# Four stationary columns for the conditioning products, all-ones input norm sums, filter operands padded to 128 rows

## What is computed

```python
def rms_norm(x, gain):
    xf = x.astype(jnp.float32)
    y = xf * lax.rsqrt(jnp.mean(xf * xf, axis=-1, keepdims=True) + NORM_EPS)
    return (y * gain.astype(jnp.float32)).astype(x.dtype)
...
def adaln(cond, ada_w, ada_b):
    m = jax.nn.silu(cond) @ ada_w + ada_b
    return jnp.split(m, 3, axis=-1)
...
    hid = jnp.sin(feats @ w1 + b1)
    hid = jnp.sin(hid @ w2 + b2)
    taps = (hid @ w3 + b3).reshape(L, 2, HY_ORDER, HY_WIDTH)
...
    yn = ((yf - mean) * lax.rsqrt(var + RWKV_GN_EPS)).reshape(y.shape[:2] + (BRANCH_W,))
    yn = (yn * gn_w + gn_b).astype(v.dtype)
```

## Time and profile before

| | |
|---|---|
| median of three runs | 3252.37 us (3250.11 to 3253.16) |
| the profiled execution | 3250.34 us, span 3248.5 us |
| PE busy | 2901.3 us, 89% |
| DVE busy | 1540.9 us, 47% |
| ACT busy | 1063.6 us, 33% |
| POOL busy | 62.1 us, 2% |
| moved by DMA | 243.24 MB, mean 75 GB/s |

### The profile page before, as it was taken

One profiled execution on the slowest core, in us unless ns is written; L12 is line 12 of the kernel. 1 busy time (PEld: TensorE's weight loads), 2 busy tenths in 40 slices (PEclk: granted clock), 3 DMA queues, 4 the chain that ended last, 5 costly groups with the idle time before them and its releaser, 6 DMA issues. The chain is left out here.

```text
span 3248.5 us, 53541 instructions
## 1 busy us (share of the span) xinstructions
PE 2901.3 (89%) x23122; PEld 2232.8 (69%) x23122; DVE 1540.9 (47%) x2528; ACT 1063.6 (33%) x1886; POOL 62.1 (2%) x69
## 2 busy tenths in 40 slices
PE   7899889989986888788999999799887988899997
PEld 3588656867855777346788777566656876788876
DVE  5623347353546555556555224454536435354522
ACT  6411357232242333212222222454324133322221
POOL 0000000000000122000000000000000000000000
PEclk9899999989976999698999999899988998899999
DMA  9411200124125111301232223222211112223321
GB/s 314 120 59 52 43 1 2 52 76 131 33 58 146 46 50 33 107 19 46 79 99 95 91 76 107 89 60 66 59 52 55 40 58 92 72 75 94 97 85 65
DMA packets 250172, 243.24 MB, mean 75 GB/s; under 512 B 28248, under 2 KB 218200, under 8 KB 249873
## 3 DMA queue, kind: packets, MB, share of 16 engines
q1 hardware_dynamic: 249634, 238.64, 23.7%
q10 hardware_dynamic: 304, 1.18, 0.1%
HBM read 217.03 MB, written 22.24 MB: 74 GB/s over the span
## 5 line engine op out<-in xcount | busy, mean ns | idle before, releaser
L212 DVE TENSOR_TENSOR second_w_low<-second_w_raw,second_w_high 128x1024 fp32r<-128x1024 f32 (+1 forms) x236 | 282.3, 1198 | 486.8 <-ACT second_w_high L208 486.0
L208 ACT CAST second_w_high<-second_w_raw 128x1024 fp32r<-128x1024 f32 (+1 forms) x236 | 241.6, 1025 | 681.0 <-PE ffn_in_acc L233 248.5
L231 PE MATMUL ffn_in_acc<-ffn_h_high,second_w_high 128*128 128x512 f32 x704 | 280.9, 399 | 7.7 <-DVE ffn_h_low L674 5.8
L233 PE MATMUL ffn_in_acc<-ffn_h_high,second_w_low 128*128 128x512 f32 x704 | 278.2, 395 | 0.0
L232 PE MATMUL ffn_in_acc<-ffn_h_low,second_w_high 128*128 128x512 f32 x704 | 278.2, 395 | 0.0
L212 DVE TENSOR_TENSOR first_w_low<-first_w_raw,first_w_high 128x1024 fp32r<-128x1024 f32 x91 | 110.7, 1223 | 248.2 <-ACT first_w_high L208 248.0
L208 ACT CAST first_w_high<-first_w_raw 128x1024 fp32r<-128x1024 f32 x91 | 94.7, 1047 | 208.5 <-PE attn_in_acc L233 80.7
L231 PEld LDWEIGHTS ffn_in_acc<-ffn_h_high,second_w_high 128*128 128x128 f32 x704 | 133.9, 190 | 39.6 <-issue 9.9
L231 PE MATMUL attn_in_acc<-attn_h_high,first_w_high 128*128 128x256 f32 (+1 forms) x416 | 144.3, 347 | 14.4 <-DVE attn_h_low L406 14.4
L232 PEld LDWEIGHTS ffn_in_acc<-ffn_h_low,second_w_high 128*128 128x128 f32 x704 | 134.0, 190 | 29.6 <-issue 0.7
L233 PEld LDWEIGHTS ffn_in_acc<-ffn_h_high,second_w_low 128*128 128x128 f32 x704 | 133.8, 190 | 29.7
(11 more groups left out here) (817 smaller groups left out, 6353.1 us busy)
## 6 DMA issues: line engine op xcount, KB each, us to landing
second_w_raw<-in_ffn_w_gate SPq DMA_DIRECT2D x44, 512.0 KB, 3.5
second_w_raw<-in_ffn_w_up SPq DMA_DIRECT2D x44, 512.0 KB, 3.6
second_w_raw<-in_ffn_w_down SPq DMA_DIRECT2D x40, 512.0 KB, 3.4
first_w_raw<-in_rec_w_in SPq DMA_DIRECT2D x33, 512.0 KB, 3.8
second_w_raw<-in_w_in SPq DMA_DIRECT2D x24, 512.0 KB, 3.8
second_w_raw<-in_w_branch_gate SPq DMA_DIRECT2D x24, 512.0 KB, 3.8
first_w_raw<-in_attn_w_in SPq DMA_DIRECT2D x22, 512.0 KB, 3.7
first_w_raw<-in_attn_ada_w SPq DMA_DIRECT2D x12, 512.0 KB, 8.4
```

What stands on the lines that cost most here:

```text
L208: act.copy(self.view(self.high[b % self.splits], b), self.view(self.raw[self.ring[b]], b)).then_inc(self.high_done, 1)
L212: dve.tensor_tensor(self.view(self.low[b % self.splits], b), self.view(self.raw[self.ring[b]], b), self.view(self.high[b % self.splits], b ...
L231: pe.matmul(out, sh, mh, start=(first and j == 0), stop=False)
L233: ins = pe.matmul(out, sl, mh, start=False, stop=(last and j == len(parts) - 1))
```

## The change

Three things change, and one moves with them.

The diff, cut to its core:

```diff
@@ class InputRoots
     def begin(self, st):
-        self.root = Root(self.nc, st, self.c, self.root_out, ring=4)
         self.squares = [st.sb(f"squares{i}", [P, TT]) for i in range(4)]
-        self.spread = st.ps("root_spread", [P, 2 * BANK])
+        self.sums = st.ps("root_sums", [P, 2 * BANK])
+        self.squared, self.summed, self.rooted = (st.sem("root_" + n) for n in ("squared", "summed", "rooted"))
...
-        if step == 16:
-            self.root.take(act)
-        if step == 22:
-            self.root.keep(act, self.spread[:, 0:TT])
...
+        if step == 17:
+            act.wait_ge(self.summed, KD)
+            act.activation(self.root_out, self.sums[:, 0:TT], ACT.Sqrt, bias=self.c["eps"]).then_inc(self.rooted, 1)
 
     def pe(self, pe, step):
-        if 8 <= step < 8 + KD:
-            self.root.add(pe, step - 8, self.squares[(step - 8) % 4])
-        if step == 19:
-            self.root.spread_over(pe, self.spread)
+        k = step - 8
+        if 0 <= k < KD:
+            pe.wait_ge(self.squared, k + 1)
+            for t0, tn in spans(TT, BANK):
+                ins = pe.matmul(self.sums[:, t0:t0 + tn], self.c["ones"], self.squares[k % 4][:, t0:t0 + tn],
+                                start=(k == 0), stop=(k == KD - 1))
+            ins.then_inc(self.summed, 1)
 
     def dve(self, dve, step):
-        if step == 18:
-            self.root.make_diag(dve)
+        if step in (18, 20, 22):
+            at = slice(128 * (step - 18), 128 * (step - 16))
+            dve.wait_ge(self.rooted, 1)
+            dve.reciprocal(self.root_out[:, at], self.root_out[:, at])
@@ def linear_tokens
+                    if stacked:
+                        half, out = slice(t0, t0 + rows // 2), ps[n % slots][:, 0:sum(widths)]
+                        for j, k in enumerate(ks):
+                            pe.matmul(out[0:rows], x(k)[:, at], high[:, j, :], start=(k == 0), stop=False, skip_group_check=True)
+                            ins = pe.matmul(out[0:rows // 2], x(k)[:, half], low[:, j, :], start=False, stop=(k == kc - 1),
+                                            skip_group_check=True)
+                        ins.then_inc(product_done, 1)
+                        continue
@@ def adaln
-        rows = keep.enter_context(nc.sbuf_tensor("adaln_rows", [2, len(layers) * 3 * D], F32))
-        high, low = (keep.enter_context(nc.sbuf_tensor("adaln_cond_" + n, [P, KD, 2], F32R)) for n in ("high", "low"))
+        rows = keep.enter_context(nc.sbuf_tensor("adaln_rows", [4, len(layers) * 3 * D], F32))
+        parts = keep.enter_context(nc.sbuf_tensor("adaln_cond_parts", [P, KD, 4], F32R))
+        high, low = parts[:, :, 0:2], parts[:, :, 2:4]
...
-                        ins = pe.transpose(ps[:, i, n, :], rows[:, at:at + P], ident[0:2, 0:2])
+                        ins = pe.transpose(ps[:, i, n, :], rows[:, at:at + P], ident[0:4, 0:4])
...
                         chain.link(dve.tensor_tensor(mod[:, :, j], ps[:, i, :, j], bias, ALU.add))
+                        chain.link(dve.tensor_tensor(mod[:, :, j], mod[:, :, j], ps[:, i, :, 2 + j], ALU.add))
@@ def hidden_loads (new), def filter_loads
+    tables = {"hidden": Ahead(nc, keep, "filt_hidden")}
+    for n, src, shape in (("w1", "hy_w1", [33, 64]), ("w2", "hy_w2", [64, 64]), ("feats", "c_feats", [33, S])):
+        tables[n] = keep.enter_context(nc.sbuf_tensor("filt_" + n, shape, F32))
+        tables["hidden"].start(tables[n][:], d[src])
...
-                          ("taps", (("w3", [65, 2, 1024]), ("decay", [P, 4, 512]))), ("transform", (("dft", [P, 2, 4, FREQ]),))):
+    for group, shapes in (("taps", (("w3", [P, 2, 1024]), ("decay", [P, 4, 512]))), ("transform", (("dft", [P, 2, 4, FREQ]),))):
...
-    tables["taps"].start(tables["w3"][64:65], d["hy_b3"].rearrange("k (r n) -> k r n", r=2))
@@ def rwkv_out_filters
-    hid, hid1, arg, turns = (spare[0:rows, 512 * i:512 * i + 512] for i, rows in enumerate((65, 64, 64, 64)))
+    hid, hid1, arg, turns = (spare[0:rows, 512 * i:512 * i + 512] for i, rows in enumerate((P, 64, 64, 64)))
...
-    plus = y[0:65, 4:6, :].rearrange("p k t -> p (k t)")
+    plus = y[:, 4:6, :].rearrange("p k t -> p (k t)")
...
-        centre, rs, spread = st.sb("centre", [P, P]), st.sb("rs", [8, S]), st.sb("spread", [8, 4 * P])
+        centre, rs, spread = st.sb("centre", [P, P]), st.sb("rs", [P, S]), st.sb("spread", [P, 4 * P])
...
+        @block.gpsimd
+        def _(pool):
+            pool.memset(w3[64:P], 0.0).then_inc(w3_cleared, 1)
+            pool.wait_ge(w3_cleared, 1)
+            pool.memset(spread[:], 0.0).then_inc(spread_cleared, 1)
+            pool.memset(rs[:], 0.0).then_inc(rs_cleared, 1)
 
         @block.sync
         def _(sp):
-            sp.dma_start(spread[:], d["c_spread2"][0:8, 0:4 * P]).then_inc(landed, 16)
+            sp.wait_ge(w3_cleared, 1)
+            sp.dma_start(w3[64:65], d["hy_b3"].rearrange("k (r n) -> k r n", r=2)).then_inc(b3_landed, 16)
+            sp.wait_ge(spread_cleared, 1)
+            sp.dma_start(spread[0:8], d["c_spread2"][0:8, 0:4 * P]).then_inc(landed, 16)
...
-            dve.memset(hid[64:65, :], 1.0)
+            dve.memset(hid[64:P, :], 0.0).then_inc(ones_row, 1)
+            dve.wait_ge(ones_row, 1)
+            dve.memset(hid[64:65, :], 1.0).then_inc(ones_row, 1)
...
             tables["taps"].wait(dve)
+            dve.wait_ge(w3_cleared, 1)
+            dve.wait_ge(b3_landed, 16)
             chain.link(dve.tensor_tensor(plus, w3[:, 0], w3[:, 1], ALU.add))
@@ def rec_layer
+            hidden = hidden_loads(nc, d, mid)
             scanned = sb("scanned", [P, 4, S], mid)
             rwkv_scan(nc, d, c, vt, ends, scanned, feats, chunk, last_saved)
...
-                tables = filter_loads(nc, d, filters)
+                tables = filter_loads(nc, d, filters, hidden)
```

More of the change, by code:

```diff
@@ L3027, in filter_loads @@
             tables[name] = tables[group].sb(name, shape)
-    for n, src in (("w1", "hy_w1"), ("w2", "hy_w2"), ("feats", "c_feats")):
-        tables["hidden"].start(tables[n][:], d[src])
     tables["taps"].start(tables["w3"][0:64], d["hy_w3"].rearrange("k (r n) -> k r n", r=2))
-    tables["taps"].start(tables["w3"][64:65], d["hy_b3"].rearrange("k (r n) -> k r n", r=2))
     tables["taps"].start(tables["decay"][:], d["c_decay"].rearrange("(a p) n -> p a n", p=P))
@@ L3171, in _ @@
             act.wait_ge(varied, 1)
-            act.activation(rs[:], stat_ps[0:8, :], ACT.Sqrt, bias=c["eps_gn"][0:8]).then_inc(rooted, 1)
+            act.wait_ge(rs_cleared, 1)
+            act.activation(rs[0:8], stat_ps[0:8, :], ACT.Sqrt, bias=c["eps_gn"][0:8]).then_inc(rooted, 1)
             for n, (o, j, t) in enumerate(taps):
@@ L3239, in _ @@
             dve.wait_ge(rooted, 1)
-            dve.reciprocal(rs[:], rs[:]).then_inc(inverted, 1)
+            dve.reciprocal(rs[0:8], rs[0:8]).then_inc(inverted, 1)
             for n in range(3):
```

30 lines of the change are left out of this document (20 added, 10 removed).

## The result

| | before | after |
|---|---|---|
| median of the runs | 3252.76 us (4 runs, 3250.11 to 3257.76) | 3232.06 us (4 runs, 3229.35 to 3238.04) |
| ratio, 95% interval | | 0.9937 [0.9918, 0.9956] |
| profiled execution's span | 3248.5 us | 3232.1 us |
| PE busy | 2901.3 us | 2867.2 us |
| DVE busy | 1540.9 us | 1544.0 us |

What follows compares the result with a forecast made beforehand. PE was taken to set the pace in the conditioning's squares and, at 1.2 GHz, to bound the late stage's taps. 4.3 - 0.8 + 0.1 + 11.0 = 14.6 us gained gave 3237 us, range 3230 to 3246.

Steps and rivals of the forecast that it cites:

- The late stage: Late stage in all: 11.0 us gained, as 3.5 at its start, 6.4 in the taps and 1.1 in the transforms.
- the padding: Late-stage taps: with 128 rows they run at full clock, rounds take 4.1 us, and the transforms come 6.4 us nearer.
- the transforms: Late-stage transforms, at half clock before: full clock would save 2.15 us; half of that, 1.1 us, was taken.
- the start: Late stage's start: the bias row lands at 1332.5, so the reciprocal ends near 1343.3 instead of 1346.77, 3.5 us gained.
- one of my signs of being wrong: Late stage: DVE's sum of the two halves (L3233) waiting past 18 us would show the prediction wrong.
- The conditioning: Conditioning stage: 3.5 us gained in blocks 8 to 15, 1.7 lost in 16 to 24, 2.5 gained after; 4.3 in all.
- The steps 2.21, 15.2 and 1.35 us: Conditioning: 2.21 us a step in blocks 8 to 15, 15.2 us for blocks 16 to 24, 1.35 a block afterwards.
- the additions: Turning stage: four additions join a chain on DVE, 0.8 us lost.
- Rival 3: Conditioning: PE partly idle, so the clock falls; 40 blocks at half clock cost 20 + 10 us, total 3267; chance 5%.
- The clears: Semaphore clears move from rwkv_feat, ffn1_in, mem_k, ffn2_in to rwkv, nsa_in, dn_scan: net 0.1 us gained, bounds -1.5 to +1.5.
- DVE's wait ahead of the scan: Boundary at rwkv: three new load issues before the barrier cost 1.6 us and the clear 0.4 to 1.0; 2.0 lost.
- 1.0 us each: Stage boundaries: one with a clear takes 1.5 us, one without 0.55, so each clear costs 1.0 us.

Runs made afterwards that it cites:

- the second trace: The kernel after, unchanged, run and traced once more beside the kernel before: 3231.99 us, ratio 0.9946 [0.9932, 0.9960].

## Why the prediction was right, and where it was not

**The late stage: the mechanism right, the size right in the padding and not in the loads.** The clock follows the padding; the narrow matmuls in an otherwise equal kernel are the proof. From the readout's reciprocal to the transforms 35.5 us became 29.2 (6.3, forecast 6.4; 6.0 in the second trace), a round is 4.10 us, the transforms lost 2.1 (forecast 1.1, bound 2.15; 1.5 in the second trace). The term that is off is the start: I took 3.5 us, and measured from the stage's start the sum of halves came 1.9 us earlier in the first trace and not at all in the second (19.6 against 19.5 us). The bias row landed later than my 1332.5, which on the scale of before is 1334.0 (I had 1331 to 1334.5) in the first trace; that 1332.52 stands in it is due to the stage starting 1.5 us earlier. In the second trace the sum waited past 18 us, one of my signs of being wrong. The terms are not independent either, as I had treated them. The early loads without padding bring 0.2 us of the 10.4, the padding without them 3.0 (94.8 to 91.8), both 10.4.

**The conditioning: the blocks right, the end wrong.** The steps 2.21, 15.2 and 1.35 us are the forecast's to a hundredth or two. Two things lay beyond them. First, the stage ends with casts for the next stage, whose small loads SP issues at 0.77 us: 1.3 us of the gain. Second, the turning: the additions cost 0.8 as said, and the 48 transposes took 5.25 instead of 4.11 us. In the second trace of after they took 4.14. There the clock fell 1.5 us after they began (1.6 before), in the first trace 0.3 us ahead of them; so the extra 1.1 us comes of the clock and not of the width.

**Rival 3 was the nearest miss, and the argument against it was wrong.** I let the clock fall because PE idles, and that is how it fell in the kernel with four columns alone, behind a wait of 1.96 us. Against it I argued that PE at half clock would be always busy, which "brought the clock back" in the earlier trace rows. It did so within 3.4 us where the squares are summed in 512 and 256 columns, and not for 37.5 us beside the one-column sums, though PE had no gap. What spared the kernel after is then twofold: its waits were shorter (1.2 and 1.5 us in its two traces), and it has the other edit, whose sums I had priced as a small loss. Neither is a step of the prediction, so that this was luck. I had costed the two edits as independent terms; they are one.

**The clears: the counting right, the price wrong in one place.** The three clears stand where I said. DVE's wait ahead of the scan grew from 4.58 to 5.98 us (6.86 in the second trace), by 1.4 and 2.3 against a forecast of 2.0. The -1.0 and +1.8 of the table agree with the forecast, but prove little: from rwkv_feat's first product to the scan's the second trace of after takes 94.9 us, which is 0.9 less than before. A clear costs 1.2 us of idle time; ahead of ffn2_in it also held the clock down for 9 to 13 us more, 5.9 us of time to the root between these two traces and 4.3 to the end. My step "1.0 us each" took the barrier alone and not what PE does at its two speeds behind it.

**The sum.** -14.6 on the scale of the traces against -16.4. Without the 4.3 that ffn2_in's half clock is worth to the end and the 2.0 of the scan (chance: other kernels with the same scan lie on both sides) it would be -10.1: the forecast was close partly by luck, because a gain that I had not seen made up for one that was not there. The likeliest reading of the change: 7.4 to 10.4 us from the late stage, some 5.5 (4.3 and 1.2) from the clear that left ffn2_in, 0.8 lost around the scan, nothing from the conditioning as it stands (some 3 if the reciprocals are hidden). That makes 12 to 15; the medians differ by 18 to 21, and the rest I can't place.

## What to carry to other kernels

A busy PE at half clock is a clue, not a fate: look at what its matmuls are, here such with few rows or with one moving column, and pad with zeros where the next engine leaves room. Before taking products out of a stage, look at the waits that PE then has and at what stays in the stage: waits let the clock fall here, and beside one-column sums it didn't come back. Cost a stage to its real end, including what it does for the next one, and put idle engines' gaps (DVE during transposes) to use before optimising the operation that would fill them.

## What was not expected of the hardware

- PE busy 37.60 of 37.60 us with 128 rows stayed at 1.2 GHz, once a wait of 1.96 us had let the clock fall, while 12 one-column passes stood between four 512-column products of 4 and 2 stationary columns; with sums of 512 and 256 columns it was back 3.4 us after such a fall. With six products and no wait (before) it stayed at 2.4 GHz (16.00 of 16.00 us busy).
- 96 rows, 31 of them zero in the taps, ran at 0.98 of the full clock in the rounds, 65 at 0.50; where the clock was still up, a round with 65 rows took the same 4.1 us.
- A float32 reciprocal takes 4.95 us for 768 columns on 128 partitions and 3.34 us for 512 on 8: 6.4 to 6.5 ns a column, on 128 partitions as on 8 (256 columns: 1.74 us, 6.8 ns).
- A clear of semaphores added 1.23 us to an idle time of 4.6, and the clock came back 12.1 to 15.8 us after the next product instead of 3.1 to 3.4.
- 48 float32 matmuls with 4 rows, 128 stationary columns and 2 moving ones took 20.10 us, 48 transposes of the same operand 4.14 to 5.25.
